# Two-layer attention network on one Trainium2 core: query layout and loads of the local attention, first row maxima of the latent attention in two groups, latent values stored as plain fp32

## What is computed

```python
for i in range(DEPTH):                       # DEPTH = 2
    y = mixers[i % 3](x, positions, *layer_params[i]) @ w_out[i]
    x = _layernorm(DEEPNORM_ALPHA * x + y, ln_g[i], ln_b[i])
    x = x + jax.nn.sigmoid(x @ pe_gate[i]) * (p[i] @ pe_proj[i])
```

## Time and profile before

| | |
|---|---|
| median of 3 runs | 3166.45 us (3164.95 to 3171.06) |
| profiled execution | 3169.97 us, its span 3168.1 us |
| PE busy | 2963.8 us, 94% of the span |
| DVE / ACT / POOL busy | 1893.9 / 1629.4 / 1430.8 us |
| DMA | 549.53 MB, mean 173 GB/s |
| largest DMA queue (SP's) | 399.62 MB |

### The profile page before, as it was taken

The page is one execution under the profiler, slowest core; times in us unless marked ns, Lnnn a source line. Parts: engine busy times, 40 slices in busy tenths (PEclk is TensorE's granted clock), DMA queues, the critical chain, the costliest instruction groups (busy, mean ns, idle before and its releaser), DMA issues. The chain is left out here.

```text
span 3168.1 us, 41018 instructions
## 1 busy us (share of the span) xinstructions
PE 2963.8 (94%) x13536; PEld 2326.5 (73%) x13536; DVE 1893.9 (60%) x2692; ACT 1629.4 (51%) x2830; POOL 1430.8 (45%) x1158
## 2 busy tenths in 40 slices
PE   7999987888999999999988699999999999899998
PEld 6888875555788788777766377777777777588876
DVE  3544313343378765555653578788787787357875
ACT  3111113557435544444554177777777777644553
POOL 0022103556222540000563088888888888623353
PEclk9999998999999999999998599999999999999999
DMA  5355449875997675554899743443533533399674
GB/s 164 82 126 119 119 136 208 203 193 165 282 293 242 216 240 179 175 168 154 272 375 337 198 98 71 101 99 71 117 83 79 119 71 101 92 305 280 223 235 147
DMA packets 297350, 549.53 MB, mean 173 GB/s; under 512 B 30976, under 2 KB 118656, under 8 KB 289984
## 3 DMA queue, kind: packets, MB, share of 16 engines
q1 hardware_dynamic: 222912, 399.62, 44.9%
q10 hardware_dynamic: 74240, 147.49, 15.4%
HBM read 366.24 MB, written 180.49 MB: 173 GB/s over the span
## 5 line engine op out<-in xcount | busy, mean ns | idle before, releaser
L2475 POOL TENSOR_TENSOR mla_pl<-mla_p,mla_ph 128x512 fp32r<-128x512 f32 (+3 forms) x640 | 707.6, 1121 | 202.8 <-ACT mla_p L2349 194.3
L1479 PE MATMUL end_bank<-end_xh,end_whi 128*128 128x512 f32 x1808 | 717.7, 397 | 45.7 <-DVE end_wlo L1710 17.9
L1480 PE MATMUL end_bank<-end_xl,end_whi 128*128 128x512 f32 x1808 | 708.3, 392 | 0.0
L1481 PE MATMUL end_bank<-end_xh,end_wlo 128*128 128x512 f32 x1808 | 707.6, 391 | 0.0
L1548 ACT CAST end_whi<-early_wraw 128x1024 fp32r<-128x1024 f32 (+1 forms) x228 | 235.0, 1031 | 578.4 <-PE end_bank L1481 527.2
L2348 ACT ACTIVATE mla_ph<-mla_score 128x512 fp32r<-128x512 f32 (+3 forms) x640 | 341.8, 534 | 225.3 <-PE mla_score L2199 217.1
L1710 DVE TENSOR_TENSOR end_wlo<-early_wraw,end_whi 128x1024 fp32r<-128x1024 f32 x188 | 254.1, 1352 | 320.1 <-ACT end_whi L1548 320.1
L1479 PEld LDWEIGHTS end_bank<-end_xh,end_whi 128*128 128x128 f32 x1808 | 342.4, 189 | 133.9 <-DVE end_wlo L1710 25.4
L2376 DVE TENSOR_REDUCE mla_mx<-mla_mx 128x1 f32<-128x512 f32 (+3 forms) x640 | 372.4, 604 | 87.6 <-PE mla_mx L2199 86.9
L2422 DVE TENSOR_TENSOR mla_acc<-mla_acc,mla_p 128x512 f32<-128x512 f32 (+3 forms) x576 | 349.2, 606 | 120.2 <-ACT mla_p L2349 115.7
L1480 PEld LDWEIGHTS end_bank<-end_xl,end_whi 128*128 128x128 f32 x1808 | 342.5, 189 | 72.8 <-issue 2.9
(11 more groups left out here) (234 smaller groups left out, 4992.1 us busy)
## 6 DMA issues: line engine op xcount, KB each, us to landing
early_wraw<-in_pe_gate ACTq DMA_DIRECT2D x64, 512.0 KB, 5.2
early_wraw<-in_w_out ACTq DMA_DIRECT2D x62, 512.0 KB, 7.2
early_wraw<-in_w_in ACTq DMA_DIRECT2D x56, 512.0 KB, 3.8
swa_q<-scratch_q_hi SPq DMA_DIRECT2D x32, 512.0 KB, 10.1
end_factor<-scratch_inv SPq DMA_DIRECT2D x64, 256.0 KB, 9.7
scratch_proj<-end_out_f SPq DMA_DIRECT2D x64, 256.0 KB, 6.6
scratch_sum<-end_out_f SPq DMA_DIRECT2D x64, 256.0 KB, 6.0
end_old<-scratch_proj SPq DMA_DIRECT2D x64, 256.0 KB, 3.6
```

The source lines that it names most:

```text
L1479: nc.tensor.matmul(bank, wh[:, at], xh[:, k0 + k, :], start=(k == 0), stop=False)
L1480: nc.tensor.matmul(bank, wh[:, at], xl[:, k0 + k, :], start=False, stop=False)
L1481: last = nc.tensor.matmul(bank, wl[:, at], xh[:, k0 + k, :], start=False, stop=(k == kc - 1))
L2475: pool.tensor_tensor(p_lo[b][:, off:TC], prob[b][:, off:TC], p_hi[b][:, off:TC].bitcast(F32), ALU.subtract).then_inc(p_lo_ok, 1)
```

## The change

It has four parts.

- **Local attention's queries.** In DRAM q0 and k0 are laid out so that high and low part and both halves of a head's rows follow one another, and rows are ordered with the head of the group innermost. A unit's first query tile is then one DMA over 128 partitions (2 MB) in place of four over 32 partitions; the second is one over 64 partitions in place of two over 32; each key tile is one DMA over 64 partitions in place of two over 32. `load_high` issues 3 DMAs in place of 8, `load_low` 3 in place of 5. Bytes and runs (4 KB a run for the queries) stay as they are; rows of neighbouring partitions are now 4 DRAM rows apart in place of one. The columns of the weights and the frequencies are ordered to suit on the host.
- **First maxima of the latent attention in two groups** (`lead`). Unit 0 does 12 of its 40 items (the rows of chunks 0 and 1) before the first score, with a gather, turn and `max_row` of their own. Its other 28 items go into slots 0 to 7, their gather into slot 8, turn and negate into slot 9, `max_row` into slot 10; chunk 2 (slot 12) waits for that row. Unit 1's items go into slots 10 to 32 of unit 0.
- **Latent values as fp32.** A v tile of stage "ukv" is copied by DVE alone into one of the 6 output tiles and stored with 256 KB. In "mla" a unit loads 512 KB of values (runs of 256 bytes in place of 512), ACT rounds them (`values_high`, 128x1024 elements) in slot 20 of the unit before, ahead of that slot's probabilities, and DVE subtracts (`values_low`) in slot 21, ahead of that slot's items. For unit 0 ACT rounds them ahead of the first `max_row`, after waiting for all of `load_low(0)`, and DVE subtracts after the first negate.
- **The ones** are written by POOL in place of DVE.

```diff
@@ chain_phase, output tiles and v tiles
-        out_tiles = [n for n, x in enumerate(tiles) if x["kind"] not in ("turn", "v")]
+        out_tiles = [n for n, x in enumerate(tiles) if x["kind"] != "turn"]
...
-                    sp.dma_start(latent["v"][x["i"], :, 4 * q + x["at"], :], v_tile(n).rearrange(
-                        "p h two d -> p (h two d)")).then_inc(v_stored[values[n] % 3], 16)
+                    sp.dma_start(latent["v"][x["i"], :, 4 * q + x["at"], :], out_f[place[n]][:]
+                                 ).then_inc(stored[place[n]], 16)
...
-                elif x["kind"] == "v":
-                    act.wait_ge(product, n + 1)
-                    wait_v_free(act, n)
-                    act.copy(v_tile(n)[:, :, 0, :].bitcast(F32R), bank.rearrange("p (h d) -> p h d", d=HEAD_DIM)
-                             ).then_inc(hi_ok, 1)
...
                 elif x["kind"] == "v":
-                    dve.wait_ge(hi_ok, highs[n])
-                    vec.tensor_tensor(v_tile(n)[:, :, 1, :].bitcast(F32R), bank.rearrange("p (h d) -> p h d", d=HEAD_DIM),
-                                      v_tile(n)[:, :, 0, :], ALU.subtract).then_inc(dve_out, 1)
+                    dve.wait_ge(product, n + 1)
+                    wait_out_free(dve, n)
+                    vec.tensor_copy(out_f[place[n]][:], bank).then_inc(dve_out, 1)
@@ attention_phase, plan of the items
+        lead = cfg["lead"]
+        late = lead["slots"] + 1 if lead else 0
+        own_share = share(0, items[0], 0, lead["slots"], lead["items"]) if lead else {}
+        shares = [share(kind, items[(kind + 1) % kinds], 0, cfg["items_to"]) for kind in range(kinds)]
+        first_share = share(0, items[1 % kinds], late + 2, cfg["items_to"]) if lead else shares[0]
...
+        turns = [(0, 0, lead["blocks"]), (0, lead["blocks"], blocks)] if lead else [(0, 0, blocks)]
+        turns += [(u, 0, blocks) for u in range(1, units)]
...
+        values_at = 20
@@ attention_phase, SP
                     if n == cfg["n_load_b"] - 1 and u >= 2:
-                        sp.wait_ge(weighed, ends[u - 2])
+                        if long:
+                            sp.wait_ge(v_lo_ok, u - 1)
+                        else:
+                            sp.wait_ge(weighed, ends[u - 2])
@@ attention_phase, PE
+                if lead and u == 0 and st["first"] and st["chunk"] * (TC // P) == lead["blocks"]:
+                    pe.wait_ge(*row_landed(1))
...
+                if long and k == 0:
+                    pe.wait_ge(v_lo_ok, u + 1)
...
-            for n in range(ni[0]):
+            for n in range(lead["items"] if lead else ni[0]):
                 item(0, n)
@@ attention_phase, ACT
+            def values_high(u):
+                act.wait_ge(ld_b[u % 2], 16 * cfg["n_load_b"] * (u // 2 + 1))
+                if u >= 2:
+                    act.wait_ge(weighed, ends[u - 2])
+                act.copy(vals[u % 2][:, :, 0:HEAD_DIM], v_raw[u % 2][:]).then_inc(v_hi_ok, 1)
...
+            if long:
+                values_high(0)
             max_row(0)
...
+                    if long and k == values_at and u + 1 < units:
+                        values_high(u + 1)
@@ attention_phase, DVE
-            for tile in k_tiles[k_ones]:
-                op = vec.memset(tile[rows:kr, :].bitcast(F32), 1.0)
-            op.then_inc(const_ok, 1)
...
+            def values_low(u):
+                dve.wait_ge(v_hi_ok, u + 1)
+                vec.tensor_tensor(vals[u % 2][:, :, HEAD_DIM:P], v_raw[u % 2][:],
+                                  vals[u % 2][:, :, 0:HEAD_DIM].bitcast(F32), ALU.subtract).then_inc(v_lo_ok, 1)
...
+                    if long and k == values_at + 1 and u + 1 < units:
+                        values_low(u + 1)
+                    for v, n in at_slot(u, k):
+                        item(v, n)
                     add(g)
@@ swa_config
-    def queries(u, tile, part, row=0):
+    def queries(u, tile, n_rows):
         g, b = divmod(u, 2)
-        src = q[part].rearrange("s g (j r) t -> s g r j t", j=GROUP)
-        for s in range(2):
-            yield (tile[row + s * 32:row + (s + 1) * 32, :].rearrange("r (j t) -> r j t", j=GROUP),
-                   src[s, g, :, :, b * half_b * P:(b + 1) * half_b * P])
+        src = q[g].rearrange("a s (r j) t -> (a s r) j t", j=GROUP)
+        return (tile[0:n_rows, :].rearrange("r (j t) -> r j t", j=GROUP),
+                src[0:n_rows, :, b * half_b * P:(b + 1) * half_b * P])
...
     def load_a(u, q_tile, k_tile):
-        yield from queries(u, q_tile, 0)
-        yield from keys(u, k_tile, 0)
-        yield from queries(u, q_tile, 1, HEAD_DIM)
-        yield from keys(u, k_tile, 0, HEAD_DIM)
+        yield queries(u, q_tile, P)
+        yield keys(u, k_tile, 0)
+        yield keys(u, k_tile, 0, HEAD_DIM)
@@ mla_config
-        yield vals[:], v[u // half_heads].rearrange("p n (h d) -> h p n d", d=P)[u % half_heads]
+        yield vals[:], v[u // half_heads].rearrange("p n (h d) -> h p n d", d=HEAD_DIM)[u % half_heads]
...
+                lead=dict(items=12, blocks=NB // 2, slots=7), here=here, first_loads=first_loads, next_loads=next_loads,
@@ build
-        q0, k0 = parts("q0", [2, KV_HEADS, P, SEQ]), parts("k0", [2, 1, P, SEQ])
+        q0, k0 = dram("q0", [KV_HEADS, 2, 2, P, SEQ]), dram("k0", [1, 2, 2, P, SEQ])
```

More of the change, by code:

```diff
@@ L1126, in chain_phase @@
         outs, olds, turns = upto("pe"), upto("wo", "pe"), upto("pe", "z")
-        highs, rotated, values = upto("split", "v"), upto("turn", "kr"), upto("v")
+        highs, rotated = upto("split"), upto("turn", "kr")
         def row_of(x):
@@ L2123, in attention_phase, with share @@
         item0 = [sum(ni[v % kinds] for v in range(u)) for u in range(units + 1)]
-        def share(kind):
-            sizes = [TC - st["off"] for st in steps[kind]][:cfg["items_to"] + 1]
-            wide = [x["groups"] * x["width"] for x in items[(kind + 1) % kinds]]
-            out, n, done, goal = [], 0, 0.0, 0.0
-            for size in sizes:
-                goal += size * sum(wide) / sum(sizes)
+        def share(kind, todo, k0, k1, n0=0):
+            sizes = [TC - st["off"] for st in steps[kind]][k0:k1 + 1]
+            wide = [x["groups"] * x["width"] for x in todo]
+            out, n, done, goal = {}, n0, 0.0, 0.0
+            for k, size in enumerate(sizes, k0):
+                goal += size * sum(wide[n0:]) / sum(sizes)
                 mine = []
-                while n < len(wide) and (done + wide[n] / 2 <= goal or len(out) == len(sizes) - 1):
+                while n < len(wide) and (done + wide[n] / 2 <= goal or k == k1):
                     mine.append(n)
@@ L2276, in _ @@
                     scored(g)
-                    for n in at_slot(u, k):
-                        item(u + 1, n)
-                    if k == turn_at and u + 1 < units:
-                        turn(u + 1)
+                    for v, n in at_slot(u, k):
+                        item(v, n)
+                    for e in turns_at(u, k, 1):
+                        turn(e)
                 if 0 <= g - lag < total:
@@ L2377, in item, with gather @@
                                   AX.X, ALU.max).then_inc(mx_done, 1)
-            def gather(u):
-                dve.wait_ge(mx_done, item0[u + 1])
-                if u:
-                    dve.wait_ge(m_turned, u)
+            def gather(e):
+                u, b0, b1 = turns[e]
+                dve.wait_ge(mx_done, item0[u] + (lead["items"] if lead and e == 0 else ni[u % kinds]))
+                if e:
+                    dve.wait_ge(m_turned, e)
                 if sinks is None:
-                    for n, (col, per, out) in enumerate(cfg["gather"]):
+                    for col, per, out in cfg["gather"]:
+                        if not b0 <= out < b1:
+                            continue
                         op = vec.tensor_reduce(m_all[:, out:out + 4],
@@ L2467, in out_gate @@
                                    ).then_inc(gated, 1)
+            for tile in k_tiles[k_ones]:
+                op = pool.memset(tile[rows:kr, :].bitcast(F32), 1.0)
+            op.then_inc(const_ok, 1)
             for g in range(total + tail):
```

127 lines of the change are left out of this document (68 added, 59 removed).

## The result

The changed kernel takes 3178.12 us (median of 6 runs, 3172.84 to 3181.39) against 3166.01 (6 runs, 3159.68 to 3172.79) for the kernel before beside it: ratio 1.0031, 95% interval 1.0019 to 1.0044 (the two medians by themselves lie 0.4% apart). It is slower by 0.3%; 3136 was predicted. The profiled execution took 3172.84 us, its span 3171.0, against 3169.97 and 3168.1.

A forecast was written before the change was run, and what follows sets the result against it. PE was taken to bound the latent units (busy 848 of 865 us), with saturated DMA and waits earlier. Terms -29 - 23 - 5 + 27 = -30 us gave 3140 profiled, 3136 against the median; whole range 3098 to 3170.

The forecast's parts named there:

- Wide query loads, -29: Local attention and the wait before it: 128-partition query loads run at 347 in place of 217 GB/s, saving 29 us.
- The head: Wait before the local attention: faster loads of units 0 and 1 save 7 us.
- the stage: Local attention itself: faster query loads of units 2 to 7 save 22 us of queue time.
- Values stored once, -23: Stage "ukv": v stores of 256 in place of 512 KB remove ACT's waits and save 23 us.
- In unit 0 ... 5 us back: Latent unit 0: unit 1's 40 items in 23 slots take DVE 38 us against PE's 33, giving 5 us back.
- start of the latent attention, -5: Latent attention's start: first score 20 us earlier, most given back; sum -5 us, between -11 and +5.
- DMA, 2.0 us: Latent attention's start: the transfer of the first row of maxima, ahead of the first score, takes 2.0 us.
- the other 28 items take DVE about 21.5 us ... plus some 4 us of adds: Latent unit 0, slots 0 to 7: DVE's items and adds end near 1815 in place of 1827, leaving 12 us.
- 14 units x 1.9 = +27 us: Latent units: rounding and subtraction in slots 20 and 21 make PE 1.9 us late each, costing 27 us.
- without what a lower clock would add: Latent units' added work: its upper bound of +43 us leaves out any loss from a lower PE clock.
- The slow rival: Latent units: 3.1 us of stall plus 1.7 of lowered clock each, 67 us in 14 units; 3177 us, chance 0.12.
- its point of decision of 4.1: Latent units: the slow rival decides from 57/14 = 4.1 us lost a unit, against three gains of 57 us.

The follow-up runs named there:

- e4: The kernel before with only the wide query loads and the ones on POOL added: 3133.5 us, ratio 0.9903.
- e3: The changed kernel with the 40 first maxima in one group ahead of the first score again: 3171.2 us, ratio 1.0025 to the kernel before.
- e2: The changed kernel with the latent values stored and loaded as two halves again: 3140.3 us, ratio 0.9926 to the kernel before.
- e5: The changed kernel with one group of first maxima, rounding at slot 33 and subtraction at slot 36: 3120.7 us, ratio 0.9856 to the kernel before.
- e8: The changed kernel with one group of first maxima, rounding at slot 35 and subtraction at slot 36: 3122.6 us, ratio 0.9865 to the kernel before.
- e1: The changed kernel with the rounding at slot 37 and the subtraction at slot 38: 3169.8 us, ratio 1.0019 to the kernel before.
- e11: The changed kernel with one group of first maxima, rounding at slot 34 and subtraction at slot 36: 3127.8 us, ratio 0.9874 to the kernel before.
- e6: The changed kernel with the subtraction cut to 1 block of 16 from the third unit on: 3142.8 us, ratio 0.9925 to the kernel before.
- e9: The changed kernel with the first row issued before unit 0's rounding, later rounding at slot 35 and subtraction at 36: 3130.4 us, ratio 0.9894 to the kernel before.

## Why the prediction was wrong

- **Wide query loads, -29: right**, 25.4 measured (near 24 as the mean over the traces). The head gave 10 rather than 7 us, the stage 15 rather than 22; two misses that partly cancel. DVE's wait for the stores fell from 56.3 to 44.5 us, not to nothing.
- **Values stored once, -23: right**, 26.4 between the local attention and the barrier, 29.0 in e4 against e3, near 24 as the mean over the traces.
- **"In unit 0 ... 5 us back"; start of the latent attention, -5: wrong**, +1.7 in the profile. Moving the ones gave 5.9 us (e4), as counted, and the two groups took it and more back. The first score came near its forecast, with two errors that cancel: the row's "DMA, 2.0 us" from the earlier trace rows had an empty queue, and this row stood behind unit 1's loads for 6.5; the wait for the values was shorter. The step that failed is "the other 28 items take DVE about 21.5 us ... plus some 4 us of adds": from ACT's first probabilities of slot 0 to those of slot 8 it took 30.6 us, not 25.5, because PE at half clock paces these slots. By slot 8 the lead was 4.4 us where 12 were forecast, and by the end of the unit it was gone. e2 shows the loss without any rounding in the way (unit 0 3.6 us longer than e4's).
- **"14 units x 1.9 = +27 us": this step failed, and it decided the sign.** The place and the mechanism were right, and the stop (1.84 + 0.20) nearly so. The term left out the clock, "without what a lower clock would add", which only a rival with a chance of 0.12 had. A unit lost 3.9 us, and 14 of them some 54: twice the term.
- **The slow rival** asked for 3.1 us of stop and 1.7 of clock; it got about 2.2 and 1.6, 3.85 together, just under its point of decision of 4.1. With 54 lost against some 52 gained the two nearly balance, and the sign turned because the start of the latent attention did not pay its 5 us. Its price for the clock, read from the one stall at 604.6 us, was right to 0.1 us. I had the figure and didn't put it in the sum: PE is the bound and idles where it never did, so the same reading belonged in the main case.
- **The duration from the earlier trace rows** was a median of 1.23 us with a maximum of 2.35. Those differ by what POOL does: of the 188, the 36 that began while a POOL instruction ran took what was left of it and 1.08 us more (one 1.17), the others 1.15 to 1.23. I used the median in a slot in which POOL is always busy, as the kernel before shows:

```profile
2018.85 5.26 POOL L2475 TENSOR_TENSOR mla_pl<-mla_p,mla_ph 128x512 fp32r<-128x512 f32 x4
```

The measured value, 1.81, was inside the bounds.
- In the medians the change costs 12 us, in the profiled executions 3. e3's profiled execution is likewise the fastest of its runs, 8 us under their median. The traces say where equal code scatters (ahead of the local attention, in it and behind it, by 4 to 9 us each), not why.

## What to carry to other kernels

On the engine that bounds a stage, a new stop of a microsecond or more can have a second price, the clock behind it (here 1.6 us, in 10 to 13 of 14 units); count it in the main case. Before placing extra work on a helper engine, find how many slots lie between it and the next thing that the bounding engine takes from there, times the slack of a slot, and compare with the work's duration beside the neighbours that it will have, on VectorE what is left of GpSimd's running instruction included: the same instructions cost 3.9 us a unit at slots 20 and 21 and 0.4 at 33 and 36. A small transfer that gates everything is best issued when the queue is empty; whether it helps to issue it ahead of the large loads, no run here tried.

## What was not expected

**One subtraction, five durations.** DVE's subtraction of 128x1024 from two tiles in SBUF, first in unit 0 of e5, where POOL is idle, then in its units at slot 36 (columns: min/median/max ns, first and last start):

```profile
L2434 DVE TENSOR_TENSOR mla_v<-mla_v_raw,mla_v x1: 1202/1202/1202, 1752.3 to 1752.3; 128x1024 fp32r<-128x1024 f32 x1
...
L2434 DVE TENSOR_TENSOR mla_v<-mla_v_raw,mla_v x14: 1965/2144/2156, 1814.4 to 2569.7; 128x1024 fp32r<-128x1024 f32 x14
```

It is 1202 ns alone, 1.61 us in e8, 1.81 at slot 21 and in e1, 1.89 in e11 and 2.14 in e5, mostly repeating to some ns within a kernel; in all but the first POOL works beside it. POOL's timeline around one of them in e5, whose subtraction runs from 1988.67 to 1990.81 us:

```profile
1988.44 1.28 POOL L2514 TENSOR_TENSOR mla_pl<-mla_p,mla_ph 128x512 fp32r<-128x512 f32 x1
1989.69 2.28 POOL L2514 TENSOR_TENSOR mla_pl<-mla_p,mla_ph 128x512 fp32r<-128x512 f32 x1
```

POOL's running instruction has 1.06 us left when the subtraction starts, and the subtraction takes 1.06 + 1.08 us. At slot 21 it is 0.73 + 1.08, in e8 0.52 + 1.09, in e11 0.81 + 1.08, and in e6, with a sixteenth of the elements, 0.73 + 0.08. So the subtraction waits for the end of POOL's instruction. What follows is 1.08 to 1.09 us for the whole tile, in every unit of every kernel with the split, a little less than the 1.20 that it takes alone. POOL's next instruction in turn takes 2.24 to 2.28 us in place of 1.28 in the kernels named (1.27 in e6). POOL's subtraction reads two SBUF tiles too. The Trainium skill (SBUF — State Buffer, "Who interferes with whom") has DVE and POOL share a pair of SBUF ports under an exclusive lock, and says that a DVE instruction with two SBUF inputs contends for it with a POOL instruction that reads SBUF, the second blocked until the first is done. The traces agree, with 0.73 us of wait at slot 21.

**A stop doesn't always cost clock.** Equal stops of 1.22 us lowered it in 10 units of 14, and longer ones not in every unit either, so a single stall read from a trace tells what a fall costs and not how often it comes. Nor are stops under a microsecond free of it. In unit 1 of e9 PE stood 0.49 and, 2.4 us later, 0.69 us, in unit 2 0.49 and 0.71. The 4 us behind each:

```profile
1821.20:1825.20 4.00, 3.98 (x13) 2.82 (x14) 1.62 (x4) 1.44 (x4) 2.88 (x4) 0.57 1.03 184
1881.40:1885.40 4.00, 4.00 (x24) 3.18 (x25) 2.30 (x5) 2.20 (x8) 3.77 (x4) 1.00 0.99 176
```

Unit 1 took 60.2 us and unit 2 58.6.
